# Two of the delta rule's 24 convolution tiles: from one VectorE sum to ScalarE products added on GpSimd

## The reference

```python
def short_conv(x, w):
    C = x.shape[-1]
    return lax.conv_general_dilated(
        x, w[:, None, :].astype(x.dtype), window_strides=(1,),
        padding=((CONV_K // 2, CONV_K // 2),),
        dimension_numbers=('NWC', 'WIO', 'NWC'), feature_group_count=C)
...
        qkv = jax.nn.silu(short_conv(jnp.concatenate([dq, dk, dv], axis=-1), conv_w[i]))
        cq, ck, cv = qkv[..., :DN_KW], qkv[..., DN_KW:2 * DN_KW], qkv[..., 2 * DN_KW:]
```

## Time and profile before

| | |
|---|---|
| median of the runs | 1669.21 us (1666.99 to 1671.65, 3 runs) |
| the profiled execution | 1670.91 us, span 1669.1 us |
| busy share of PE, DVE, ACT, POOL | 89%, 40%, 23%, 18% |
| the convolution's loop | about 387 to 587 us |
| DVE adding taps in it (L2364) | 96 instructions, 71.9 us |
| mean granted TensorE clock | 0.959 of 2.4 GHz |

### The profile page before, as it was taken

One profiled execution on the slowest core, in us unless ns is written; L12 is line 12 of the kernel. 1 busy time (PEld: TensorE's weight loads), 2 busy tenths in 40 slices (PEclk: granted clock), 3 DMA queues, 4 the chain that ended last, 5 costly groups with the idle time before them and its releaser, 6 DMA issues. The chain is left out here.

```text
span 1669.1 us, 22426 instructions
## 1 busy us (share of the span) xinstructions
PE 1478.6 (89%) x8686; PEld 995.7 (60%) x8686; DVE 675.9 (40%) x1203; ACT 380.5 (23%) x814; POOL 296.7 (18%) x261
## 2 busy tenths in 40 slices
PE   5998998999999978988999999999988968887782
PEld 5864445884544457777888778674657854332320
DVE  3321435124369956775232154310363444332224
ACT  3213445104333333321110132301231010000001
POOL 0020011620007244563540000000000002111110
PEclk9999999999999979999999999999988978999996
DMA  6128210213112213434322030322133066999994
GB/s 208 49 81 261 68 51 26 84 43 126 51 51 76 64 64 126 130 131 136 101 86 92 1 126 26 78 64 79 38 93 127 1 241 238 422 425 425 424 388 170
DMA packets 118385, 228.27 MB, mean 137 GB/s; under 512 B 13202, under 2 KB 102896, under 8 KB 109332
## 3 DMA queue, kind: packets, MB, share of 16 engines
q1 hardware_dynamic: 112963, 216.34, 36.0%
q0 software_dynamic: 5184, 8.55, 1.4%
q10 hardware_dynamic: 144, 2.10, 0.3%
HBM read 221.56 MB, written 15.74 MB: 142 GB/s over the span
## 5 line engine op out<-in xcount | busy, mean ns | idle before, releaser
L917 PE MATMUL psv<-arena 128*128 128x256 f32 x800 | 175.8, 379 | 2.7 <-ACT arena L1681 1.3
L882 PE MATMUL psv<-arena,wslot 128*128 128x512 f32 x384 | 170.8, 598 | 1.8 <-DVEq L2154 1.8
L917 PEld LDWEIGHTS psv<-arena 128*128 128x128 f32 x800 | 151.6, 190 | 25.3 <-issue 4.9
L1586 ACT ACTIVATE arena<-pss 128x512 f32<-128x512 f32 (+1 forms) x157 | 84.8, 540 | 333.1 <-PE pss L882 275.2
L882 PE MATMUL pss<-wslot,arena 128*128 128x256 f32 (+1 forms) x640 | 147.6, 391 | 4.6 <-issue 2.0
L882 PE MATMUL pss<-arena 128*128 128x256 f32 (+1 forms) x512 | 141.7, 434 | 6.3 <-ACTq L151 3.1
L1504 PE MATMUL pss<-arena 128*64 128x512 f32 x384 | 123.9, 655 | 18.8 <-DMA arena<-w_expert_in 16.4
L882 PEld LDWEIGHTS pss<-wslot,arena 128*128 128x128 f32 x640 | 120.7, 190 | 30.3 <-issue 11.8
L882 PEld LDWEIGHTS pss<-arena 128*128 128x128 f32 x512 | 95.9, 190 | 45.6 <-issue 29.8
L882 PEld LDWEIGHTS psv<-arena,wslot 128*128 128x128 f32 x384 | 71.1, 190 | 85.5 <-issue 83.0
L2364 DVE SCALAR_TENSOR_TENSOR arena<-psv,ccols,arena 128x510 f32<-128x510 f32 (+1 forms) x96 | 71.9, 749 | 59.9 <-ACT arena L1737 56.8
(11 more groups left out here) (339 smaller groups left out, 1977.6 us busy)
## 6 DMA issues: line engine op xcount, KB each, us to landing
arena<-w_expert_in SPq DMA_DIRECT2D x24, 2048.0 KB, 18.3
wslot<-w_in SPq DMA_DIRECT2D x32, 1024.0 KB, 5.4
arena<-w_expert_out SPq DMA_DIRECT2D x32, 1024.0 KB, 18.8
wslot<-w_ada SPq DMA_DIRECT2D x18, 1024.0 KB, 5.2
wslot<-w_expert_in SPq DMA_DIRECT2D x8, 2048.0 KB, 16.0
arena<-w_in SPq DMA_DIRECT2D x10, 1024.0 KB, 8.7
arena<-w_ada SPq DMA_DIRECT2D x6, 1024.0 KB, 7.9
arena<-x SPq DMA_DIRECT2D x8, 512.0 KB, 8.6
```

Source lines behind the costliest of these rows:

```text
L882: m = mm(o, l, r, start=(n == 0), stop=(n == len(pairs) - 1))
L917: m = mm(o[:, j * HALF_T:(j + 1) * HALF_T], l[:, c, j * P:(j + 1) * P], r[:, c, :], start=new and j == 0 and c == 0, stop=j == 1 and c == ...
L1586: L.did(A(dst, src, func, **kw), s[sig] if sig else None, [s["free_s"]])
```

## The change

For the value tiles j = 20 and j = 22, ACT makes all five products: after the middle tap it multiplies the four shifted windows of the bank by their taps into a new buffer `far` and raises `whole_ready`. POOL adds the four into `conv[:, j % 2]` (`convolve`), and its last add raises `far_ready`, for which ACT's SiLU now waits. DVE does not add anything for these two tiles: it waits for `whole_ready` and raises `free_v`. POOL's two calls stand ahead of `key_decay(0)` and behind `intra_mask(0)`. `far` lies in SBUF that is otherwise used for the squares of the keys and queries. Three semaphores that nothing used are taken out of the list of names.

```diff
+        far = at(D + 8 * K, 4, SEQ)
...
+        FAR_CONV = (20, 22)
...
                     L.did(A(conv[:, j % 2, :], psv[:, conv_job(j) % 4, :], ACT.Copy, scale=tap(j, 2)), s["tap_ready"])
+                    if j in FAR_CONV:
+                        if j > FAR_CONV[0]:
+                            act.wait_ge(s["far_ready"], FAR_CONV.index(j))
+                        for k in (0, 1, 3, 4):
+                            m = k - 2
+                            lo, hi = max(0, -m), SEQ - max(0, m)
+                            ins = A(far[:, k - k // 3, lo:hi], psv[:, conv_job(j) % 4, lo + m:hi + m], ACT.Copy, scale=tap(j, k))
+                            if k < 4:
+                                L.go(ins)
+                            else:
+                                L.did(ins, s["whole_ready"])
...
-                    L.need(s["conv_ready"])
+                    if j in FAR_CONV:
+                        act.wait_ge(s["far_ready"], FAR_CONV.index(j) + 1)
+                    else:
+                        L.need(s["conv_ready"])
...
+            def convolve(n):
+
+                j = FAR_CONV[n]
+                pool.wait_ge(s["whole_ready"], n + 1)
+                for k in (0, 1, 3, 4):
+                    m = k - 2
+                    lo, hi = max(0, -m), SEQ - max(0, m)
+                    o = conv[:, j % 2, lo:hi]
+                    L.did(TT(o, o, far[:, k - k // 3, lo:hi], ALU.add), s["far_ready"] if k == 4 else None)
+
+            convolve(0)
             key_decay(0)
             intra_mask(0)
+            convolve(1)
             diagonal(0)
...
-                for k in (0, 1, 3, 4):
+                if j in FAR_CONV:
+                    dve.wait_ge(s["whole_ready"], FAR_CONV.index(j) + 1)
+                    L.raise_(s["free_v"])
+                for k in () if j in FAR_CONV else (0, 1, 3, 4):
```

More of the change, by code:

```diff
@@ L453, in build @@
             rs_in rs_out atok_ready rope_ready qkT_ready negmax_ready probs_ready probsn_ready pT_ready
-            oT_ready tmp_ready tmp_used oz_ready ga_ready ga_step gg_ready gG_ready conv_ready silu_ready
-            half_ready row_ready sq_ready rt_ready norm_ready on_ready dz_ready mixT_ready mo_ready
+            oT_ready oz_ready ga_ready ga_step gg_ready gG_ready conv_ready silu_ready
+            half_ready row_ready sq_ready on_ready dz_ready mixT_ready mo_ready
             x1_ready x1T_ready pinT_ready sg_ready x2_ready mod_ready h2_ready hc_ready p2_ready mT_ready
@@ L464, in build @@
                 tte_ready tt_ready vb_ready r_ready vn_ready kdec_ready st_ready o_ready at_pre at_ready sum_ready qs_ready tap_ready rk_in rk_out bt_ready
-                part_ready term_ready mid_ready held_ready add_ready raw_ready corner_ready gate_ready""".split():
+                part_ready term_ready mid_ready held_ready add_ready raw_ready corner_ready gate_ready whole_ready far_ready""".split():
             s[n] = sem(n)
```

## The result

The changed kernel takes 1673.47 us in the median (22 runs), the kernel before 1668.85 us (22 runs in all). The ratio is 1.0025, with a 95% interval of 1.0018 to 1.0032. The two medians lie 4.6 us apart. The forecast was +4.2 us. The profiled execution's span is 1673.8 us.

The account below looks back on a forecast made before the run. PE bounds the whole kernel, but DVE sets this stage's end. Terms -0.97 (given back), +3.51 (tile 20) and +1.68 (tile 22) sum to +4.2 us: 1673.4 us from a median of 1669.21, range 1669.4 to 1676.0.

Parts of the forecast that it names:

- What bounds the stage: From tile 18 on, DVE's gapless work to its last product at 592.26 sets the end; a microsecond there is one of the kernel.
- The order of ACT's stream: Middle tap of the next tile queues behind the SiLU waiting for POOL: chain 10.78 us, 1.30 and 1.68 longer than before.
- POOL's adds: Four dependent adds per moved tile at 1.27 us each, 5.29 us with gaps of 0.07.
- ACT's products: Four products per moved tile, overlapping as they are issued without a wait: 2.49 us, or 2.85 without overlap.
- Exclusion in SBUF: Beside tile 20, one small DVE step per POOL instruction, six in a row: 12.99 us, so tile 21 3.51 late.
- Given back: Behind tile 18, the decay product no longer delays DVE's first elimination step at 552.65: 0.97 us earlier.
- At nothing: Earlier raise of `free_v`, removed names and the new buffer cost nothing.
- Rival 1: No mutual exclusion in tile 20, or cheaper adds: +2.0 or +2.4 us, with both +0.2; chance 0.17.
- Rival 2: DVE's steps also delay POOL's adds in tile 20: +5.8 us, or 6.6 if ACT's products don't overlap; chance 0.23.
- Rival 3: DVE alone sets the pace and the work simply leaves it: -7.5 us, 1661.7; chance 0.04.
- Rival 4: PE's clock falls as PE idles some 5 us instead of 4.25: less than 1 us; chance 0.02 of over 1.

Follow-up runs that it names:

- only22: Changed kernel with only tile 22 on ACT and POOL, decay and mask products at their old place; 1672.20 us, ratio to kernel before 1.0027; repeated 1670.37 us, 1.0012.
- only20: Changed kernel with only tile 20 on ACT and POOL, decay and mask products behind POOL's adds; 1672.56 against 1668.12 us for the kernel before, ratio 1.0029.
- steps_late: Changed kernel with DVE's elimination steps 24 to 27 moved behind the adds of tile 21; 1670.15 against 1668.12 us for the kernel before, ratio 1.0013.
- mask_first: Changed kernel with POOL's decay and mask products put back ahead of its adds for tile 20; 1671.59 against 1668.12 us for the kernel before, ratio 1.0023.
- decay_on_steps: Kernel before, DVE adding for all tiles, with POOL's decay and mask products held until tile 20's SiLU is done; 1669.50 against 1668.31 us, ratio 1.0006.
- all_three: Changed kernel with the edits of tap_early, steps_late and mask_first together; 1667.30 against 1668.31 us for the kernel before, ratio 0.9994.
- tap_early: Changed kernel with ACT's middle tap of tile j + 1 right behind its products of j, ahead of the SiLU; 1669.50 against 1668.31 us for kernel before, ratio 1.0003.
- half_projections: all_three with half of the input channels left out of PE's projections of tiles 22 and 23; 1666.23 us in a single run, not compared.

## Why the prediction was right, point by point

- **What bounds the stage.** DVE's last product was taken as the stage's end, and a microsecond there as one of the kernel. The stretch grew by 4.01 us. The first matmul behind the barrier came at 601.38 instead of 596.48: of these 4.90 us, 0.89 had arisen before the stretch began. The part behind took 1072.4 us against 1072.6, but as that part scatters by several us between traces, the times are the better evidence that nothing was made up there. In eight of ten comparisons (the change, the eight kernels of the experiments that do the full work, one of them twice) the medians differ from the kernel before by what the stretch says, within 0.8 us; the two others are the first only22 and only20.
- **The order of ACT's stream.** The chain was priced 10.78 us; it is 10.80 us for tile 22 with the change, 10.80 in only22 and 10.67 for tile 20 in steps_late. The agreement to 0.02 us is in part luck: the products took 0.07 less than priced and the hops between engines 0.08 more (0.44 instead of 0.36), above all that from ACT to DVE, 0.13 instead of 0.05. With the middle tap moved ahead of the SiLU the gap falls to 8.22. So it is this order, not the number of instructions on ACT, that makes tile 23 late.
- **POOL's adds.** Priced 1.27 each after L1970, they take 1.266 in the median, four 5.29 to 5.30 us, as in the sum. The estimate from the 2.6 cycles per element of the Trainium skill (GPSIMD Engine Reference, section Performance versus the Vector engine) had been 1.11 without dispatch, 0.16 us below the measurement.
- **ACT's products.** Four were priced at 2.49 us; they take 2.42 together. The overlap of instructions that don't wait was read rightly from L1791 and is a little larger, about 0.11 us for each instead of 0.09.
- **Exclusion in SBUF.** Six steps of 1.25 to 1.31, one for each of POOL's six instructions in a row; forecast gap 12.99, measured 12.72. The largest part of the 0.27 is the last term, a hop of 0.16 in front of tile 21's adds, which is 0.04 in the trace (574.69 to 574.73); POOL also started 0.10 earlier than priced, and the sixth step's end follows POOL's by 0.15 and not 0.22. mask_first (four long steps) and decay_on_steps (two, with none of the change's new work in the kernel) show that it depends on POOL's instructions beside the steps and on nothing else of the change. The transposes beside POOL's second four adds took 4.04 us, against 4.11 before the change. The adds of taps, which read PSUM, took their 3.10 us at 572.36 in steps_late with POOL's mask product at 572.31 beside them, and at 569.23 in all_three with POOL's own adds beside them. With the rule of the Trainium skill, GPSIMD Engine Reference, section Key points, on shared SBUF interfaces the traces agree: steps with two SBUF inputs wait, the transposes and the adds from PSUM don't.
- **Given back.** 0.97 us by the decay product that no longer meets the step at 552.65: measured 0.97 (6.50 to 5.53), and again, within 0.02, in only20, steps_late, tap_early and decay_on_steps, not in only22, mask_first and all_three, where the product is at its old place.
- **At nothing.** The diff removes four semaphore names, not three. The parts above leave nothing of the stretch for them or for the earlier `free_v`.
- **The rivals.** Rival 1 (no exclusion or cheaper adds) fell with the six long steps. Rival 2 (POOL held up by DVE) fell as well: with steps of DVE between them POOL's four adds take 5.29 us together. Rival 3 (the work simply leaves DVE) is wrong in the change, and even in all_three only 1.7 of the 6.5 us come out. There PE's last projection sets tile 23, as half_projections shows, but it explains only 0.9 of the 4.8 us that are missing. The rest can be read from the rows of half_projections, though no run removes it: DVE waits 1.21 us for ACT ahead of tile 21 and 1.76 ahead of the transposes, and one small step is held by POOL for 0.94 longer; 39.77 - 6.52 + 3.91 = 37.16 us, against a measured stretch of 37.15. Rival 4 (the clock) cost nothing visible on the chain. PE did not idle once for some 5 us but 4.50 and 2.91 us, ahead of the turns of tiles 22 and 23. The granted clock was 0.81 of full in 585 to 590 and 0.50 in 590 to 595, and the turn of tile 22 took 1.71 us where that of tile 21 had taken 1.09, but behind it PE waited again. The four groups of instructions between the last product's end and the barrier took 4.22 us in both traces (596.48 - 592.26 and 601.38 - 597.16).
- **The size.** The stretch grew by 0.2 us less than forecast: 0.27 less in tile 20, 0.06 more elsewhere. That the median, 1673.47, lies within 0.1 us of the forecast 1673.4 is luck: the medians of the kernel before alone moved from 1669.21 to 1668.85.

What stays open: the times of the first only22 and of only20 lie some 2 us above their stretches. For only22 a repetition came out near its stretch; for only20 there was none. And what all_three would gain without its last waits for ACT and POOL was not measured.

## What to carry to other kernels

Work moved off the busiest engine comes out only if no instruction that the busy engine waits for stands, in the order of a third engine's stream, behind the moved work: count the new chain through all streams, and compare it with what the busy engine has left to do, not with what was taken from it. Look also at what the moved work will run beside: beside a GpSimd instruction of 1.27 us a VectorE step of 0.3 us with two SBUF inputs took about 1.3. Two such instructions fewer in GpSimd's row shortened the gap around tile 20 by 1.94 us in mask_first, and the stretch by 0.97, as the other 0.97 was lost again behind tile 18. And where a stage is short, measure it by a stretch in the trace that begins behind the scatter: it told about 0.1 us, where a dozen runs told about 2.

## What the runs showed of the hardware

A small VectorE step with two SBUF inputs that meets a GpSimd instruction of 1.27 us with SBUF inputs ends only behind it, whatever its own size: 128x175 elements took 1.25 instead of 0.34 us, 128x31 took 1.29 instead of 0.19. In a row of GpSimd instructions one such step got through for each: six of six with the change, four of four in mask_first, two of two in decay_on_steps. GpSimd was hardly held in return: four adds took 5.28 or 5.29 us with a small step held behind each, 5.29 with nothing of DVE beside them (tile 20 in steps_late), and 5.30 to 5.32 beside the transposes. They took 5.35 for tile 22 in steps_late, and 5.41 for tile 20 in all_three, where a step of 0.34 us had begun at 572.49, 0.09 us ahead of the fourth add, and that add took 1.37 instead of 1.27.
